# Attention stage of a streaming encoder step: three PSUM banks in one ring, a shift of one rounded row, and fewer mask casts on GpSimd

## The reference, cut to what matters

```python
logits = einsum('bqhgd,bqkhd->bqhgk', qg, k_sel) * HEAD_DIM ** -0.5
logits = where(valid, logits + bias, -inf)
p = softmax(logits, axis=-1)
o = einsum('bqhgk,bqkhd->bqhgd', p, v_sel)
```

## Time and profile before

| what | before |
|---|---|
| median of 3 runs | 3721.62 us (3712.66 to 3726.58) |
| span of the profiled execution, from the first to the last instruction | 3720.7 us |
| PE busy, share of the span | 3443.0 us, 93% |
| DVE busy, share of the span | 2743.4 us, 74% |
| ACT busy, share of the span | 1436.8 us, 39% |
| POOL busy, share of the span | 1185.7 us, 32% |

### The profile page before, as it was taken

The page is one execution under the profiler, slowest core; times in us unless marked ns, Lnnn a source line. Parts: engine busy times, 40 slices in busy tenths (PEclk is TensorE's granted clock), DMA queues, the critical chain, the costliest instruction groups (busy, mean ns, idle before and its releaser), DMA issues. The chain is left out here.

```text
span 3720.7 us, 49529 instructions
## 1 busy us (share of the span) xinstructions
PE 3443.0 (93%) x18839; PEld 2917.5 (78%) x18839; DVE 2743.4 (74%) x4245; ACT 1436.8 (39%) x1774; POOL 1185.7 (32%) x1017
## 2 busy tenths in 40 slices
PE   5988999999998999999959999999899998989998
PEld 1888888999998999999935555555565568989887
DVE  1432888989898799999858887887777775576343
ACT  2211667979700000010035555555455551234121
POOL 2222112543343000000035634743644334655300
PEclk9999998999999999999979999999999999999999
DMA  8175437455556533444433012112011106657443
GB/s 287 53 230 199 125 120 162 158 169 175 187 182 231 183 136 141 159 160 160 149 70 69 25 36 63 33 32 68 24 33 31 32 20 208 203 199 240 154 141 116
DMA packets 386301, 480.19 MB, mean 129 GB/s; under 512 B 49086, under 2 KB 307278, under 8 KB 385617
## 3 DMA queue, kind: packets, MB, share of 16 engines
q1 hardware_dynamic: 321041, 269.39, 24.8%
q10 hardware_dynamic: 54976, 171.17, 13.1%
q0 software_dynamic: 10112, 37.49, 2.6%
HBM read 296.97 MB, written 187.02 MB: 130 GB/s over the span
## 5 line engine op out<-in xcount | busy, mean ns | idle before, releaser
L1069 PE MATMUL psum<-ha,gt 128*128 128x352 f32 x8136 | 1356.3, 325 | 13.0 <-DVE gq_lo L1277 8.0
L1069 PEld LDWEIGHTS psum<-ha,gt 128*128 128x128 f32 x8136 | 1326.7, 189 | 17.5 <-issue 10.1
L1340 DVE SCALAR_TENSOR_TENSOR cv<-cv,vecs,cv 128x1056 f32<-128x1056 f32 (+1 forms) x480 | 598.9, 1331 | 0.0
L1912 DVE TENSOR_TENSOR at_plo<-at,at 128x1024 fp32r<-128x1024 f32 (+2 forms) x308 | 401.7, 1305 | 134.9 <-ACT at L1808 133.8
L1807 ACT ACTIVATE at<-psum 128x1024 f32<-128x1024 f32 (+2 forms) x308 | 293.1, 952 | 493.0 <-PE psum L1689 493.0
L1734 PE MATMUL psum<-at,at 128*128 128x512 f32 (+5 forms) x688 | 337.0, 496 | 108.7 <-DVE at L1888 29.5
L663 PE MATMUL psum<-br,br 128*128 128x352 f32 x2304 | 390.5, 331 | 30.4 <-DVE br L2273 16.3
L663 PEld LDWEIGHTS psum<-br,br 128*128 128x128 f32 x2304 | 384.0, 193 | 34.6 <-issue 17.8
L737 DVE TENSOR_SCALAR_CACHE_REDUCE gl<-gt,gl 128x1792 bf16<-128x1792 f32 (+8 forms) x263 | 337.7, 1349 | 1.2
L1190 ACT ACTIVATE gt<-psum 128x1056 f32<-128x1056 f32 x80 | 84.0, 1050 | 619.0 <-PE psum L1069 597.1
L708 ACT ACTIVATE gl<-gt,gl 128x2048 bf16<-128x2048 f32 (+6 forms) x224 | 314.0, 1404 | 16.0 <-DVE gl L753 12.5
(11 more groups left out here) (255 smaller groups left out, 4901.8 us busy)
## 6 DMA issues: line engine op xcount, KB each, us to landing
scratch_ws<-gt SPq DMA_DIRECT2D x112, 512.0 KB, 4.0
gt<-scratch_ws ACTq DMA_DIRECT2D x110, 512.0 KB, 4.8
gt<-in_w_in_dram SPq DMA_DIRECT2D x60, 512.0 KB, 5.7
scratch_gm<-gt ACTq DMA_DIRECT2D x32, 528.0 KB, 3.0
br<-scratch_gm ACTq DMA_DIRECT2D x32, 528.0 KB, 3.8
scratch_m<-br POOLq DMA_DIRECT2D x32, 528.0 KB, 5.7
at<-scratch_q SPq DMA_DIRECT2D x128, 128.0 KB, 2.9
su<-in_ada_w_dram SPq DMA_DIRECT2D x6, 2048.0 KB, 22.5
```

Source lines behind the costliest of these rows:

```text
L1069: return nc.tensor.matmul(of[:, j, 0:W // 3], part[:, c, :], a[:, c, j * (W // 3):(j + 1) * (W // 3)], start=(c == 0 and k == 0), stop=(c ...
L1340: ins = nc.vector.scalar_tensor_tensor(to[:, 0:width], mine[:, k_:k_ + width], tap, to[:, 0:width], ALU.mult, ALU.add)
L1912: nc.vector.tensor_tensor(plo[j % 3][:, 0:len(mine), 0:n], prob[j % 3][:, 0:len(mine), 0:n], phi[j % 3][:, 0:len(mine), 0:n].bitcast(F32), ...
```

## The change

The ring has three banks, 5, 6 and 7. The shift no longer has a bank of its own; it takes its turn in the ring (`plan.turn`), and `plan.former` names for each turn the one three before, which must be done: by DVE, or, where that was a shift, by ACT's copy. `negate` is one instruction, which writes the negated largest, rounded, straight into `zs`; the column with the rest of the rounding is gone, and with it one row of the low products. POOL casts the mask part only for the first two heads of a unit: the other two find it in their buffer.

```diff
+    RING = 3
...
-        self.slot = {}
+        self.slot, turns = {}, []
         for s in self.steps:
+            turns += [("max",) + x for x in self.chunks_at[s]] + [("shift", u) for u in self.shift_at[s]]
             for key in ([("max",) + x for x in self.chunks_at[s]] + [("rows", u) for u in self.rows_at[s]]
                         + [("cols", u) for u in self.cols_at[s]]):
                 self.slot[key] = len(self.slot)
+            turns += [("rows", u) for u in self.rows_at[s]] + [("cols", u) for u in self.cols_at[s]]
+        self.turn = {key: n for n, key in enumerate(turns)}
+        self.former = {key: turns[n - self.RING] for n, key in enumerate(turns) if n >= self.RING}
...
-        acc, zbank, ring = mem.bank(4), mem.bank(5), [mem.bank(6), mem.bank(7)]
+        acc, ring = mem.bank(4), [mem.bank(5 + k) for k in range(plan.RING)]
...
-            return ring[plan.slot[key] % 2]
+            return ring[plan.turn[key] % plan.RING]
...
-                    if width > n:
+                    if width > n and h < 2:
                         nc.gpsimd.tensor_copy(near[e % 2][:, 0:width - n], masks[:, o:o + width - n])
...
-                nc.tensor.matmul(dst, k2[g % 2][0:HD + 2, keys], q2[u % 3][0:HD + 2, 0:n], start=False, stop=False)
+                nc.tensor.matmul(dst, k2[g % 2][0:VW, keys], q2[u % 3][0:VW, 0:n], start=False, stop=False)
...
             def ring_free(key):
-                r = plan.slot[key]
-                if r >= 2:
-                    pe.wait_ge(s_ring, r - 1)
+                former = plan.former.get(key)
+                if former is not None and former[0] == "shift":
+                    pe.wait_ge(s_aux, former[1] + 1)
+                elif former is not None:
+                    pe.wait_ge(s_ring, plan.slot[former] + 1)
...
-                pe.wait_ge(s_zlo, u + 1)
-                if u >= 1:
-                    pe.wait_ge(s_aux, u)
+                pe.wait_ge(s_neg, u + 1)
+                ring_free(("shift", u))
                 for h in range(GROUP):
-                    last = nc.tensor.matmul(zbank[0:VW + 1, h * n:(h + 1) * n], zs[u % 2][:, h, :], ident_r[:, 0:n], start=True, stop=True)
+                    last = nc.tensor.matmul(bank(("shift", u))[0:VW, h * n:(h + 1) * n], zs[u % 2][:, h, :], ident_r[:, 0:n], start=True, stop=True)
...
-                    nc.scalar.copy(q2[u % 3][HD:HD + 2, 0:n], zbank[HD:HD + 2, 0:n]).then_inc(s_aux, 1)
+                    nc.scalar.copy(q2[u % 3][HD:VW, 0:n], bank(("shift", u))[HD:VW, 0:n]).then_inc(s_aux, 1)
...
                 if h == 0 and c == 0 and u >= 2:
-                    dve.wait_ge(s_neg, 2 * (u - 1))
+                    dve.wait_ge(s_neg, u - 1)
...
-                if u >= 2:
-                    dve.wait_ge(s_zlo, u - 1)
-                nc.vector.tensor_reduce(neg[:, u % 2, :], mx[:, u % 2, :, 0:n], axis=AX.X, op=ALU.max, negate=True).then_inc(s_neg, 1)
-                dve.wait_ge(s_neg, 2 * u + 1)
                 if u >= 2:
                     dve.wait_ge(s_zp, u - 1)
-                nc.vector.tensor_copy(zs[u % 2][:, :, HD], neg[:, u % 2, :]).then_inc(s_neg, 1)
-                dve.wait_ge(s_neg, 2 * u + 2)
-                nc.vector.tensor_tensor(zs[u % 2][:, :, HD + 1], neg[:, u % 2, :], zs[u % 2][:, :, HD].bitcast(F32), ALU.subtract).then_inc(s_zlo, 1)
+                nc.vector.tensor_reduce(zs[u % 2][:, :, HD], mx[:, u % 2, :, 0:n], axis=AX.X, op=ALU.max, negate=True).then_inc(s_neg, 1)
```

More of the change, by code:

```diff
@@ L1464, in attention_stage @@
                            + [([P, 2, P], F32)] * 5
-                           + [([P, GROUP, VW + 1], F32R)] * 2
+                           + [([P, GROUP, VW], F32R)] * 2
                            + [([P, Q4], BF16), ([P, P], F32R)]
-                           + [([P, 2, GROUP, 4], F32), ([P, 2, GROUP], F32), ([P, 2, GROUP], F32)])
+                           + [([P, 2, GROUP, 4], F32), ([P, 2, GROUP], F32)])
         masks_, kst, k2, vst, vraw = parts[0], parts[1:3], parts[3:5], parts[5:7], parts[7]
@@ L1475, in attention_stage @@
         zs, ident4, ident_r = parts[41:43], parts[43], parts[44]
-        mx, neg, rinv = parts[45:48]
+        mx, rinv = parts[45:47]
         plo = [nc.alloc_sbuf_tensor_at(f"at_plo{i}", [P, 2, 512], F32R, offset=mem.at[f"at{22 + i}"]) for i in range(3)]
@@ L1485, in attention_stage @@
         s_rp, s_ring, s_S, s_phi, s_plo, s_pv = (sem(n) for n in ("rp", "ring", "S", "phi", "plo", "pv"))
-        s_neg, s_zlo, s_zp, s_aux, s_acc, s_ri, s_gate = (sem(n) for n in ("neg", "zlo", "zp", "aux", "acc", "ri", "gate"))
+        s_neg, s_zp, s_aux, s_acc, s_ri, s_gate = (sem(n) for n in ("neg", "zp", "aux", "acc", "ri", "gate"))
         POOL_SET, DVE_SET = 4, 5
@@ L1829, in _ @@
                 nc.vector.memset(kst[b][:, KEYS:KPAD].bitcast(F32), 0.0).then_inc(s_pad, 1)
-            nc.vector.memset(k2[0][HD:HD + 2, :].bitcast(F32), 1.0).then_inc(s_set, 1)
+            nc.vector.memset(k2[0][HD:VW, :].bitcast(F32), 1.0).then_inc(s_set, 1)
             half = FRONT
@@ L1841, in _ @@
                 nc.vector.tensor_tensor(kst[0][low, cols], kst[0][low, cols].bitcast(F32), ktmp0[low, cols].bitcast(F32), ALU.subtract).then_inc(s_ktmp, 1)
-            nc.vector.memset(k2[1][HD:HD + 2, :].bitcast(F32), 1.0).then_inc(s_set, 1)
+            nc.vector.memset(k2[1][HD:VW, :].bitcast(F32), 1.0).then_inc(s_set, 1)
             dve.wait_ge(s_set, POOL_SET + DVE_SET)
```

## The result

The changed kernel takes 3621.7 us (median of 4 runs, 3619.3 to 3627.6), against 3721.0 us for the kernel before (median of 4 runs beside it). The ratio is 0.974 (95% interval 0.9725 to 0.9759), about 96 us less. The forecast was 3646 with a range from 3602 to 3696.

What follows compares the result with a forecast made beforehand. PE was taken to set attention's pace, losing 102.1 us in ring waits for DVE. Bank 70, casts 1 and clock 5 us summed to 76, giving 3646 us, range 3602 to 3696 (the forecast's own 3625 to 3665).

Steps and rivals of the forecast that it cites:

- rival A: All ring waits vanish except in the sample units and the clock never falls: 111 us gained, 3611 us; chance 0.18.
- the sign of 25 to 40 us: PE's weight loads for chunks of maxima should wait 25 to 40 us for DVE's ring work instead of 102.
- The third bank: PE's ring waits for DVE: three quarters of 93 us would go, 70 us, leaving long waits' excess and bursts.
- The sample units: Three of four units where DVE lacks time to catch up (busy 16.5 of 17.4 us): about 9 us of waits stay.
- Two DVE instructions fewer: L1873 and L1875 removed, 65.7 us of DVE, 23 undisturbed: no own term; alone bounded 0 to 23 us.
- The lock: VectorE and GpSimd share a port pair: L1912 might be held instead, making relief 23 us, the sum about 10 smaller.
- Half the casts: 120 POOL casts dropped, 64 us, not on the path: 6 us of DVE, path 0 to 6, taken as 1.
- The clock: Six stage stretches at 1.2 GHz, 24 us together, cost at most 12 us: 5 us regained, between 0 and 12.
- The shift in the ring: The 68 shifts take ring turns; the third turn after one waits for ACT's copy: cost taken 0.
- Rival D: PE waits for ACT's late copy at the shift, 82 us: 57 us slower, 3778 us; chance 0.03.
- B: DVE stays behind, so PE waits one turn later; over 70 us of waits stay: 25 us gained, 3697; chance 0.20.
- C: The shift's turns eat the bank, or PE waits for exponentials: 3715 us; sign, new waits of scores or values; chance 0.07.

Runs made afterwards that it cites:

- e3_bank: Kernel before with only the ring of three banks, which the shift shares (two rows of shift, all casts): ratio 0.9814 to before, 69 us gained.
- e4_bank_row: Changed kernel with the mask part cast for all four heads again: 3633.2 us, ratio 0.9777 to the kernel before.
- e12_casts: Changed kernel, a unit's first maximum waiting only for the rounded queries, and all four casts back: median 3615.7 us, ratio 0.9728 to the kernel before.
- e11_qhi: Changed kernel, a unit's first maximum waiting only for the rounded queries, measured a second time: median 3605.5 us, ratio 0.9711 to the kernel before.
- e2_cast: Kernel before with the mask part cast for only two heads of four: ratio 0.9983 to before, 6 us gained.
- e7_qhi: Changed kernel in which a unit's first maximum waits only for the rounded queries, not the low part too: 3606.0 us, ratio 0.9709 to the kernel before.
- e5_two: Changed kernel with a ring of two banks that the shift shares: 3687.5 us, ratio 0.9923 to the kernel before.

## Why the prediction was right, point by point

The direction, the engine and the mechanism held, and the time lies in the range. It came out 24 us under the forecast, between its own range (3625 to 3665) and rival A (3611). Term by term, 70 for the bank, 1 for the casts and 5 for the clock stand against 69 for the bank, 14 for the row on top of it and 13 for the casts on top of both, with the clock's part inside them: the gap lies in the row and the casts.

- **What bounds the kernel.** Right. PE's waits for the ring were the 102.1 us that could be had; 91 are gone and the stage is 88 us shorter. In the waits that is rival A's extent, and the sign of 25 to 40 us was missed on the good side; the time stayed above A's because other waits remained or grew.
- **The third bank.** Taken as 70 of 93 us, with DVE's relief in it; `e3_bank` alone measured 69. Right in size, but for a partly different reason. Ring waits fell by more than I took, 82 us; 9 us came back as waits for POOL's queries and 8 as waits for the shift's column. That the two came out alike is partly luck. I had not named what would be late next: the list of new waits that I gave (L1814, L1808, L1912) left out POOL's L1631, which stood at 10.7 us in the trace of before.
- **The sample units.** Wrong. I left 9 us with them because DVE was busy 16.5 of 17.4 us. The one shown became 2.3 us shorter, its ring waits fell from 3.1 to 1.1 us, and DVE's busy time from 16.5 to 14.6 us; DVE is still busy nearly all of the 15.1 us. What shortened its work are the two instructions that the change removes: L1873 and L1875 took 3.1 us in this window, and the five subtractions L1912 took 1.4 us more after it (3.4, then 4.8). The case that I gave for them, "DVE is simply out of time", left out that the change itself gives DVE time (rows of the two windows, before and after):

```profile
L1912 DVE TENSOR_TENSOR at_plo<-at,at 128x512 fp32r<-128x512 f32 x5 | 3.4, 683 | 0.0
...
L1873 DVE CAST at<-at 128x4 fp32r<-128x4 f32 x2 | 2.2, 1092 | 0.1
...
L1875 DVE TENSOR_TENSOR at<-at,at 128x4 fp32r<-128x4 f32 x2 | 0.9, 460 | 0.1
```

```profile
L1912 DVE TENSOR_TENSOR at_plo<-at,at 128x512 fp32r<-128x512 f32 x5 | 4.8, 968 | 0.0
```

- **Two DVE instructions fewer.** This is a term that was mis-sized. That it "has no term of its own" was wrong: alone it is worth 18 us and on top of the bank 14. My bounds of 0 to 23 us for it held; I had taken the low end because I counted it as part of the three quarters. It acts in two ways, and I had seen only the first: DVE is less late for the ring (13.9 us of waits alone, 7.2 on top of the bank), and the shift is ready sooner (4.4 and 8.9 us).
- **The lock.** The prediction left open whether L1912 would be held in place of the removed instructions. It was, in part: with the row alone L1912 grew by 20 us (401.7 to 421.6), and with the row on top of the bank by 21 (411.2 to 432.5). So about half of the 43 us of standing still passed on, and 46 of the 65.7 us were relief, midway between the 23 and the 65.7 of the prediction. In the changed kernel L1912 stands at 426.3 us, but that holds other things too: the bank alone made it 9.5 us longer, and fewer casts made it 6 us shorter. The Trainium skill ("SBUF — State Buffer", who interferes with whom) states that a VectorE instruction with two inputs in SBUF contends with a GpSimd instruction that reads SBUF, and that a reduce never contends; the trace agrees with both. The reduce, now writing into `zs`, never took over 174 ns. The second row below is the whole subtraction of the changed kernel:

```profile
L1875 DVE TENSOR_REDUCE at<-at x68: 151/167/174, 1882.6 to 2965.5; 128x4 fp32r<-128x12 f32 x20, 128x4 fp32r<-128x4 f32 x16, 128x4 fp32r<-128x16 f32 x16, 128x4 fp32r<-128x8 f32 x16
```

```profile
L1912 DVE TENSOR_TENSOR at_plo<-at,at 128x1024 fp32r<-128x1024 f32 (+2 forms) x308 | 426.3, 1384 | 153.2 <-ACT at L1814 151.5
```

- **Half the casts.** Taken as 1 us, measured 6 alone and 13 with the rest, each with its wide interval. That POOL's casts disturb L1912 was right. I took 6 us of DVE; L1912 is 6.2 us longer in `e4_bank_row` than in the changed kernel and 9.4 in `e12_casts` than in `e11_qhi`, but only 0.8 us in before than in `e2_cast`. The step that failed is "so it is not on the path". POOL idles before these casts because it waits for DVE; what counts is when it is done with the fourth head, for the queries of the next unit stand right behind, and PE waits for them. An idle time before an instruction says nothing about what queues after it.
- **The clock.** Taken as 5 us from half of 24 us at 1.2 GHz; the changed kernel has 13.6 us left, which is a gain of 5 us at most. The size was right. But the waits that I named are not the ones that remain, since both stretches left follow a wait for POOL. And the size is partly luck: one profile of `e4_bank_row` has 34.0 us at half clock, one of `e3_bank` 10.2.
- **The shift in the ring.** Taken as 0, and 0 it is: nothing waited for L1820 in the changed kernel, 3.3 us even with two banks. Rival D's mechanism exists: with the copy 1.74 us later, PE waits 19.1 us for it, where D had 82 us for a copy as late as two exponentials can make it.
- **Rivals B and C** are out. With the bank alone 19.8 us of ring waits stay, where B needed over 70. Of C's signs the scores never waited for L1814, and the values waited 2.2 us for L1912.

## What to carry to other kernels

Where two engines go round a few buffers and the waits are about as long as one turn, one more buffer removes nearly all of them, provided that the second engine has idle time; read the mean wait against the time between two turns. Taking small instructions off that second engine still pays, here 14 to 18 us for 46 us of its time; look for what else waits for their result. A third engine's idle time ahead of a step does not make that step free: look at who waits for what it does next. And let a wait ask only for what the instruction reads: the value that `e7_qhi` changes by one was worth as much as the whole change in casts.

## What was not expected of the hardware

Stretches at 1.2 GHz, 3.4 to 10.2 us long, came inside a stage where PE is over 90% busy. After the first scores of the kernel before, of the changed kernel, of `e3_bank` and of `e4_bank_row`, each came during or within 1.5 us of a single idle time of PE's weight loads of 1.7 to 3.2 us (2.51 and 2.57 us in the changed kernel, 3.08 in one of before). Not every such wait was followed by one: `e5_two` had 81.2 us of ring waits, the longest 2.9 us, and one stretch of 3.4 us in the whole stage. None was left in `e7_qhi`, where the longest wait for another engine in the list is 1.9 us. They were worth up to 17 us (34.0 us at half clock in `e4_bank_row`).

The hold that 128x4 instructions had suffered beside POOL, 43 of the 65.7 us of busy time in 136 instructions that need 0.17 us each, passed on by about half (20 to 21 us) to the next two-input instruction when they were taken out.
